# Attention scores as two 64-row groups on TensorE, with a weight ring one slot shorter

## The chip, the core and the metric

One core of one Trainium2 chip runs the whole kernel. The metric is device time in microseconds (us), from the start of the program to its end. The kernel before took 2022.97 us (median of three runs, 2017.64 to 2026.39).

## What is computed

Two layers of a transformer-like block over 512 latent and 256 context tokens, all in fp32. The part that matters here is the attention of the second and third head group. Each has four query heads of 64 and two key/value heads (kv) that two query heads each share; the heads that share one are called r = 0 and 1.

```
q, k = rope(rms_norm(heads(...)))             # per head; context tokens are not rotated
s = q k^T / 8                                 # latent tokens see latent and context keys
p = softmax(s)                                # group 1 (windowed): +-128 tokens around, context keys, a sink term
o = p v
```

Group 0 reads all 512 latent keys and the 256 context keys. Group 1 reads the latent keys of its own tile of 128 and of the neighbouring tiles (masked to the window), and the context keys. Context queries (layer 0 only) read context keys. Around the attention stand: modulation vectors from `w_mod` (24 matrix chunks, both layers, all in layer 0), an input projection `w_in`, convolutions, the output projection `w_out`, a router, and 32 experts per layer with `e_gate`, `e_up`, `e_down`.

## The kernel before

Tokens are cut into NT = 6 tiles of 128: four latent (0 to 3), two context (4, 5). Every engine has its own program, and semaphores order them.

**Weights.** A ring of SLOTS = 6 slots of 2 MB holds the weight chunks. SyncE (SP, lines 419 to 451) loads them strictly in the order of `CHUNKS`. Load j first waits until chunk j - 6, which held its slot, is used up (`used`, line 381). A `mod` chunk serves one step and a `w_in` chunk several: columns 768 (conv steps 0 to 3), columns 0 (steps 4 to 7), columns 512 (steps 8 and 9, 1 MB), columns 1280 (q/k/v of group 0, six units) and columns 1792 (group 1, six units). The order of steps in layer 0 is made in `steps_before_attention` (lines 67 to 80): four mod steps, ten conv steps, twelve qkv units, with mod steps dealt out beside them. Below, c0 to c9 are the conv steps in order, q0 to q11 the qkv units (q0 to q5 group 0, q6 to q11 group 1), and m0 to m23 the mod steps. Behind the chunks come nine expert pieces (three experts, three matrices each): six take the ring's slots, three take late slots.

**q and k.** `qkv_projection` (line 527) makes one tile's q, k, v. `rotate` (line 954, VectorE) normalises and rotates q and k into `qk`. Then `qk_transposes` (line 514) turns it, two transposes for q and one for k, into PSUM bank 6 or 7 by turns. `store_qk` (line 1006) copies to `qT` and `kT`: 128 partitions hold the two kv halves.

**Attention.** A unit is one query tile, group, kv and r. There are 48 units in layer 0 and 32 in layer 1, and two with the same kv make a pair. For a unit, TensorE runs `scores` (S): the 128-partition q against `kT_pad`, keys in which the other half's 64 partitions are zero. Lines 574 (latent keys), 576 (masks) and 577 (context keys) do this. VectorE takes the maximum (line 1040). ScalarE takes the exponential (1463). TensorE transposes (T, line 589), ScalarE copies them out (1478), and TensorE weighs the values (W, line 605, column tiles of 64) for both units of the pair, then turns the inverse sums (X, line 611). The order on TensorE is T(u), S(u+2), T(u+1), S(u+3), W, X, T(u+2). `kT_pad` is made by GpSimd memsets (1612, 1613) and four ScalarE copies (`pad_keys`, line 1480), two of them ahead of the first exponential and two behind the second.

**Experts.** Each block of up to 64 rows multiplies with its expert's three matrices (line 728), while SyncE reloads pieces (`reload`, line 405) as experts finish.

Of the kernel before, what the change touches and what calls it, by code (L numbers as in the profile page):

```python
# [13 lines left out]
P = 128  # L14
# [43 lines left out]
SLOTS = 6  # L58
SLOT = 4096
# [7 lines left out]
def steps_before_attention(layer):  # L67

    conv = [("conv", ct) for ct in CONV_ORDER]
    qkv = [("qkv", u) for u in range(QKV_UNITS)]  # L70
    if layer:
        return conv + qkv

    mod = [("mod", n) for n in range(12 * DEPTH)]
    steps, mod = mod[:MOD_FIRST], mod[MOD_FIRST:]
    for n, step in enumerate(conv + qkv):
        beside = 2 if n == 9 else 0 if n in (14, 15, 21) else 1
        steps += [step, *mod[:beside]]
        mod = mod[beside:]
    return steps  # L80
# [3 lines left out]
MOD_CONV = MOD_FIRST + 11  # L84
# [32 lines left out]
def chunk_slot(layer, j):  # L117

    return (TURN[layer] + j) % SLOTS


def piece_slot(layer, kind, third):

    n = PIECES.index((kind, third))
    return (TURN[layer] + len(CHUNKS[layer]) + n) % SLOTS if n < SLOTS else n

# [24 lines left out]
def hybrid_flow_block(nc, x, ctx_tokens, conditions, consts, smalls, rows, w_mod, w_in, w_out, w_router,  # L151
                      e_gate, e_up, e_down, out):
    stack = ExitStack()
    with stack:
# [42 lines left out]
        kT_pad = r1[:, 3072:6144].rearrange("p (g kv t) -> p g kv t", g=2, kv=2)  # L197
# [10 lines left out]
        qk_tmp = r2[:, 5088:5472]  # L208
        ln_std = r2[:, 3072:3072 + TOK]
# [11 lines left out]
        qT = r3[:, 1536:4608].rearrange("p (i t) -> p i t", i=4)  # L221
        kT = r3[:, 4608:6144].rearrange("p (i t) -> p i t", i=2)
# [61 lines left out]
        keys_zeroed, keys_padded = sems("keys_zeroed"), sems("keys_padded")  # L284
# [26 lines left out]
        def key_tiles(layer, group, i):  # L311

            if i >= XT:
                return 0, 0
            return (0, XT) if group == 0 else (max(i - 1, 0), min(i + 2, XT))
# [56 lines left out]
        def _(sp):  # L372
# [46 lines left out]
            for layer in range(DEPTH):  # L419
                n_chunks = len(CHUNKS[layer])  # L420
                for j in range(n_chunks):
                    if j >= SLOTS:
                        sp.wait_ge(*used(layer, j - SLOTS))
                    elif layer:
                        kind, third = PIECES[j]
                        if kind == "gate":
                            end = blocks_up_to(NE // HELD * HELD + third)
                        sp.wait_ge({"gate": gate_psum, "up": up_psum, "down": y_psum}[kind][layer - 1], end)
                        if j == 1:

                            for i in range(tiles_of(layer - 1)):
                                sp.wait_ge(y_loaded[i], 16 * layer)
                    load_chunk(layer, j)
                tiles = tiles_of(layer)
                for n, (kind, third) in enumerate(PIECES):

                    if n < SLOTS:
                        sp.wait_ge(*used(layer, n_chunks + n - SLOTS))
                    elif n == SLOTS:
                        sp.wait_ge(out_psum[layer], 2 * tiles)  # L440
                    elif n == SLOTS + 1:
                        sp.wait_ge(logit_psum[layer], tiles)
                        sp.wait_ge(h2_stored[layer], 16 * tiles)
                    else:
                        sp.wait_ge(route_done[layer], 1)
                    load_piece(layer, kind, third, third)
# [8 lines left out]
        def _(pe):  # L455
# [58 lines left out]
            def qk_transposes(layer, u):  # L514
# [3 lines left out]
                if u >= 2:  # L518
                    pe.wait_ge(qkT_ready, QKV_UNITS * layer + u - 1)
# [3 lines left out]
                for r in range(2 if is_full(layer, i) else 0):  # L523
                    pe.transpose(ps[:, 6 + u % 2, r * P:(r + 1) * P], qk[:, r * P:(r + 1) * P], ident)
                pe.transpose(ps[:, 6 + u % 2, 2 * P:3 * P], qk[:, 256:384], ident).then_inc(qkT_psum, 1)
# [32 lines left out]
            def scores(layer, u, unit):  # L558
                i, group, kv, r = unit
                a, b = key_tiles(layer, group, i)  # L560
                w = (b - a) * P
                q = qT[:, group * 2 + r, i * P:(i + 1) * P]
# [3 lines left out]
                if u == 0 or u == 4:  # L566
                    pe.wait_ge(keys_padded[layer], 2 * (group + 1))
                if w:
                    masks = []
                    if group == 1 and i > 0:  # L570
                        masks.append((512 - w, cst("mask_prev")))
                    if group == 1 and i < XT - 1:
                        masks.append((512 - P, cst("mask_next")))
                    pe.matmul(ps[:, bank, 512 - w:512], q, kT_pad[:, group, kv, a * P:b * P], start=True, stop=not masks)  # L574
                    for m, (at, mask) in enumerate(masks):
                        pe.matmul(ps[:, bank, at:at + P], ident, mask, start=False, stop=m == len(masks) - 1)
                pe.matmul(ps[:, bank + 1, 0:C], q, kT_pad[:, group, kv, S:TOK], start=True, stop=True).then_inc(s_psum[layer], 1)  # L577

            def attend(layer, u, unit, last_pT):
                i, group, kv, r = unit  # L580
                a, b = key_tiles(layer, group, i)
                tiles = list(range(a, b)) + list(range(XT, NT))
                w = (b - a) * P
# [3 lines left out]
                for n in range(len(tiles)):  # L587
                    at = 512 - w + n * P
                    mm = pe.transpose(ps_flat[:, 2048 + at:2048 + at + P], prob[:, u % 2, at:at + P], ident)  # L589
                mm.then_inc(pT_psum[layer], 1)  # L590

            def weigh(layer, pair, unit):
# [3 lines left out]
                a, b = key_tiles(layer, group, i)  # L596
                tiles = list(range(a, b)) + list(range(XT, NT))
                w = (b - a) * P
# [3 lines left out]
                for n, t in enumerate(tiles):  # L602
                    at = 512 - w + n * P
                    for r in range(2):
                        mm = pe.matmul(ps[r * HD:(r + 1) * HD, 6 + pair % 2, 0:P],  # L605
                                       v_tok[:, t, group * P + kv * HD:group * P + (kv + 1) * HD],
                                       probT[:, r, at:at + P], start=(n == 0), stop=(n == len(tiles) - 1),
# [208 lines left out]
        def _(ve):  # L816
# [137 lines left out]
            def rotate(layer, u):  # L954
# [17 lines left out]
                if full:  # L972
# [10 lines left out]
                if full:  # L983
# [20 lines left out]
                nc.vector.tensor_tensor(qk[:, :], qk[:, :], qk_tmp[:, :], ALU.add).then_inc(qk_ready, 1)  # L1004

            def store_qk(layer, u):
# [3 lines left out]
                bank = ps[:, 6 + u % 2, 0:384].rearrange("p (r t) -> p r t", r=3)  # L1010
                if is_full(layer, i):
                    own(nc.vector.tensor_copy(qT[:, group * 2:group * 2 + 2, i * P:(i + 1) * P], bank[:, 0:2, :]))
                nc.vector.tensor_copy(kT[:, group, i * P:(i + 1) * P], bank[:, 2, :]).then_inc(qkT_ready, 1)
# [19 lines left out]
            def unit_max(layer, u, unit):  # L1033

                i, group, kv, r = unit
                a, b = key_tiles(layer, group, i)
                w = (b - a) * P
                base = (u % 2) * 1024
                ve.wait_ge(s_psum[layer], u + 1)
                own(nc.vector.tensor_reduce(stat[:, u % 4, 3:4], ps_flat[:, base + 512 - w:base + TOK], AX.X, ALU.max))  # L1040
# [298 lines left out]
        def _(ac):  # L1339
# [113 lines left out]
            def unit_exp(layer, u, unit):  # L1453
                i, group, kv, r = unit
                a, b = key_tiles(layer, group, i)
                w = (b - a) * P
# [6 lines left out]
                nc.scalar.activation(prob[:, u % 2, 512 - w:TOK], ps_flat[:, base + 512 - w:base + TOK], ACT.Exp,  # L1463
# [7 lines left out]
            def unit_pT(layer, u, unit):  # L1471
                i, group, _, _ = unit
                a, b = key_tiles(layer, group, i)
                w = (b - a) * P
# [3 lines left out]
                nc.scalar.copy(probT[:, u % 2, 512 - w:TOK], ps_flat[:, 2048 + 512 - w:2048 + TOK]).then_inc(pT_ready[layer], 1)  # L1478

            def pad_keys(layer, group):  # L1480

                ac.wait_ge(qkT_ready, QKV_UNITS * layer + NT * (group + 1))
                ac.wait_ge(qkv_psum, QKV_UNITS * layer + QKV_UNITS)
                ac.wait_ge(keys_zeroed[layer], 4)
                for half, kv in ((slice(0, HD), 0), (slice(HD, P), 1)):
                    nc.scalar.copy(kT_pad[half, group, kv, :], kT[half, group, :]).then_inc(keys_padded[layer], 1)  # L1486
# [111 lines left out]
        def _(po):  # L1598
# [5 lines left out]
            for layer in range(DEPTH):  # L1604
# [5 lines left out]
                po.wait_ge(qkv_psum, QKV_UNITS * layer + QKV_UNITS)  # L1610
                for group in range(2):
                    nc.gpsimd.memset(kT_pad[HD:P, group, 0, :], 0.0).then_inc(keys_zeroed[layer], 1)
                    nc.gpsimd.memset(kT_pad[0:HD, group, 1, :], 0.0).then_inc(keys_zeroed[layer], 1)
# [156 lines left out]
```

## Time and profile before

| | us |
|---|---|
| median of three runs | 2022.97 |
| the profiled execution | 2015.68 |
| its span in the trace | 2013.9 |
| layer 0: steps before attention | 0 to 311 |
| layer 0: attention | 311 to 431 |
| layer 0: experts | 583 to 1081 |
| layer 1: attention | 1290 to 1385 |
| layer 1: experts | 1493 to 1974 |
| mean granted TensorE clock | 0.941 of 2.4 GHz |

The profile has a page (busy times, the span in slices, the chain of work that ended last) and a trace that answers by window, line or tile. PE is TensorE's matmul, PEld its weight loads, DVE is VectorE, ACT ScalarE, SPq SyncE's DMA queue. An fp32 matmul stands in the trace as two LDWEIGHTS and two MATMUL records. The chain gives, for each piece, its start, its duration and what it was, with "xN" records. It follows backwards what released each step, so work that is not on it was covered by other work.

### The profile page before, as it was taken

The page shows a single profiled execution, that of the slowest core. Times are in us where ns is not written, and L with a number is a line of the kernel's source. Part 1 is how long each engine was busy: PE and PEld are TensorE (multiplying, and loading weights), DVE is VectorE, ACT ScalarE, POOL GpSimd, SP SyncE. Part 2 cuts the span into 40 slices and gives each one's busy share as a digit, 9 for nine tenths or more (in the row PEclk, how much of TensorE's full clock was granted, in tenths as well). Part 3 has the DMA queues.
Part 4 walks back from the last instruction along what each step waited for, and adds up shares of the span by engine and source line. Part 5 has one row for each costly group of instructions (what it writes and reads, how often), then busy time and mean ns, then how long its engine had stood idle before and what let it go on. Part 6 is the DMA issues. An engine that isn't in the chain of part 4 may idle for free.

```text
span 2013.9 us, 26260 instructions
## 1 busy us (share of the span) xinstructions
PE 1688.8 (84%) x9986; PEld 997.4 (50%) x9987; DVE 625.6 (31%) x1413; ACT 357.3 (18%) x730; POOL 224.8 (11%) x342
## 2 busy tenths in 40 slices
PE   4999998989869889998793699799959879777771
PEld 2555445754645556654462344475536546444430
DVE  2093655652431111110013477563331101100003
ACT  3111116641200000000002301463210000000001
POOL 0000000000001111111113100000001111111113
PEclk9999998999869999999997799899969999999996
DMA  9459246001449999899998421100359999999994
GB/s 355 153 188 344 90 150 251 2 1 52 178 167 425 427 427 427 347 428 427 427 425 338 166 104 64 42 2 1 152 204 423 426 428 427 427 427 426 428 427 161
DMA packets 85416, 541.83 MB, mean 269 GB/s; under 512 B 6544, under 2 KB 9264, under 8 KB 60784
## 3 DMA queue, kind: packets, MB, share of 16 engines
q1 hardware_dynamic: 68016, 481.51, 58.3%
q0 software_dynamic: 17344, 59.55, 7.5%
q8 instruction: 38, 0.62, 0.1%
q14 instruction: 18, 0.15, 0.0%
HBM read 515.08 MB, written 25.95 MB: 269 GB/s over the span
## 4 chain that ended last, share of the span: by engine, by line
PE 61%; DMA 27%; DVE 6%; ACT 3%; issue 2%; POOL 0%; POOLq 0%; ACTq 0%; DVEq 0%
PE ps L728 21%; DMA ring<-in_e_up_dram 14%; DMA ring<-in_e_down_dram 10%; PE ps L510 9%; PE ps L539 7%; PE ps L679 6%; PE ps L574 2%; PE ps L469 2%; PE ps L605 2%; PE ps L589 2%; PE ps L577 2%; PE ps L721 1%; PE ps L478 1%; PE ps L658 1%; DMA xres<-in_ctx_tokens_dram 1%
## 5 line engine op out<-in xcount | busy, mean ns | idle before, releaser
L728 PE MATMUL ps<-ring,r 128*64 128x256 f32 (+1 forms) x3920 | 542.1, 432 | 92.6 <-DMA ring<-in_e_up_dram 38.7
L728 PEld LDWEIGHTS ps<-ring,r 128*64 128x64 f32 x3920 | 317.7, 140 | 303.2 <-issue 149.4
L1282 DVE TENSOR_TENSOR r<-r,ps 128x256 f32<-128x256 f32 x71 | 29.9, 421 | 830.1 <-PE ps L728 830.1
L728 PE MATMUL ps<-r 128*64 128x256 f32 (+1 forms) x1760 | 239.9, 426 | 35.9 <-DMA r<-in_e_up_dram 14.7
L728 PEld LDWEIGHTS ps<-r 128*64 128x64 f32 x1760 | 142.3, 138 | 125.9 <-issue 61.3
L510 PE MATMUL ps<-r,ring 128*128 128x512 f32 (+1 forms) x480 | 176.2, 527 | 3.3 <-ACT r L1373 3.3
L1537 ACT COPY r<-ps 128x512 f32<-128x512 f32 x71 | 41.6, 585 | 669.8 <-PE ps L728 669.8
L539 PE MATMUL ps<-ring,r 128*128 128x512 f32 (+1 forms) x384 | 155.9, 560 | 0.0
L679 PE MATMUL ps<-ring,r 128*128 128x512 f32 x320 | 141.5, 598 | 2.2 <-ACT r L1508 2.2
L510 PEld LDWEIGHTS ps<-r,ring 128*128 128x128 f32 x480 | 90.9, 191 | 92.0 <-issue 84.4
L539 PEld LDWEIGHTS ps<-ring,r 128*128 128x128 f32 x384 | 71.4, 190 | 79.1 <-issue 75.0
L947 DVE SCALAR_TENSOR_TENSOR r<-r,small 128x512 f32<-128x512 f32 (+1 forms) x180 | 104.6, 661 | 0.0
L679 PEld LDWEIGHTS ps<-ring,r 128*128 128x128 f32 x320 | 60.3, 192 | 73.4 <-issue 70.7
L1626 POOL DMA_INDIRECT r<-h_dram,idx_gather x75 | 74.1, 988 | 55.0 <-POOL idx_gather L1623 55.0
L1040 DVE TENSOR_REDUCE stat<-ps 128x1 f32<-128x768 f32 (+3 forms) x80 | 60.3, 754 | 59.8 <-PE ps L577 58.6
L1634 POOL DMA_INDIRECT y_dram<-r,idx_scatter x71 | 71.1, 1002 | 57.5 <-POOL idx_scatter L1631 54.9
L1623 POOL COPY idx_gather<-list_gather 128x1 uint32 (+1 forms) x75 | 13.7, 183 | 529.5 <-PE ps L721 468.7
L469 PE MATMUL ps<-ring,cond 128*32 128x512 f32 x384 | 49.6, 637 | 23.3 <-DMA ring<-in_w_mod_dram 23.3
L1463 ACT ACTIVATE r<-ps,stat 128x768 f32<-128x768 f32 (+3 forms) x80 | 60.2, 753 | 41.3 <-DVE stat L1043 26.3
L1534 ACT ACTIVATE r<-ps 128x256 f32<-128x256 f32 x71 | 27.2, 383 | 225.2 <-PE ps L728 225.1
L574 PE MATMUL ps<-r 128*128 128x512 f32 (+2 forms) x128 | 60.4, 555 | 7.8 <-ACT r L1486 7.8
L589 PE MATMUL ps<-const,r 128*128 128x128 f32 x368 | 55.9, 282 | 12.3 <-ACT r L1478 6.1
(184 smaller groups left out, 1453.6 us busy)
## 6 DMA issues: line engine op xcount, KB each, us to landing
ring<-in_e_gate_dram SPq DMA_DIRECT2D x44, 2048.0 KB
ring<-in_e_up_dram SPq DMA_DIRECT2D x44, 2048.0 KB, 42.4
ring<-in_e_down_dram SPq DMA_DIRECT2D x44, 2048.0 KB, 31.2
ring<-in_w_mod_dram SPq DMA_DIRECT2D x24, 2048.0 KB, 18.6
r<-in_e_gate_dram SPq DMA_DIRECT2D x20, 2048.0 KB
r<-in_e_up_dram SPq DMA_DIRECT2D x20, 2048.0 KB
r<-in_e_down_dram SPq DMA_DIRECT2D x20, 2048.0 KB
ring<-in_w_in_dram SPq DMA_DIRECT2D x8, 2048.0 KB, 20.8
```

Source lines behind the costliest of these rows:

```text
L469: mm = pe.matmul(ps[32 * g:32 * g + 32, mod_bank(n), :], cond[:, 2 * g + k, :], w[:, 2 * g + k, :], start=(k == 0), stop=(k == 1), tile_po ...
L510: mm = pe.matmul(ps[:, (ct % 2) * 2 + j, 0:tn], w[:, k, col:col + P], h1T[:, t0 // P:(t0 + tn) // P, k, :], start=(k == 0), stop=(k == KD ...
L539: mm = pe.matmul(ps[:, 4 + u % 2, c0:512], h1T[:, i, k, :], chunk_ap(layer, n)[:, k, c0:512], start=(k == 0), stop=(k == KD - 1))
L574: pe.matmul(ps[:, bank, 512 - w:512], q, kT_pad[:, group, kv, a * P:b * P], start=True, stop=not masks)
L589: mm = pe.transpose(ps_flat[:, 2048 + at:2048 + at + P], prob[:, u % 2, at:at + P], ident)
L679: mm = pe.matmul(ps[:, u % 2, :], catT[:, k, i * P:(i + 1) * P], w[:, k, :], start=(k == 0), stop=(k == 7))
L728: mm = pe.matmul(ps[g * B:(g + 1) * B, bank, 0:width], x, w[:, k, g * width:(g + 1) * width], start=(k == 0), stop=(k == last), tile_posit ...
L947: ins = nc.vector.scalar_tensor_tensor(out=dst, in0=src, scalar=wt, in1=dst, op0=ALU.mult, op1=ALU.add)
L1040: own(nc.vector.tensor_reduce(stat[:, u % 4, 3:4], ps_flat[:, base + 512 - w:base + TOK], AX.X, ALU.max))
L1463: nc.scalar.activation(prob[:, u % 2, 512 - w:TOK], ps_flat[:, base + 512 - w:base + TOK], ACT.Exp, bias=stat[:, u % 4, 0:1], scale=SCALE, ...
L1626: po.indirect_dma_start(out=xg, out_offset=None, in_=h2_dram[layer], in_offset=bass.IndirectOffsetOnAxis(ap=idx_gather[:, 0:1], axis=0),). ...
L1634: po.indirect_dma_start(out=y_dram[layer], in_=y_rows, in_offset=None, out_offset=bass.IndirectOffsetOnAxis(ap=idx_scatter[:, 0:1], axis=0 ...
```

## The change

- `scores` uses 64 rows of the array at a time. Even key tiles (0, 4, 2) lie in `kT` on the kv's own half of the partitions, odd ones (1, 5, 3) on the other half. Two matmuls, one per half, write neighbouring PSUM banks. `kT_pad`, its memsets and copies, and their semaphores go.
- Every q head must lie on both halves. `rotate` writes each head twice into `q_twice` (512 columns), there are four transposes for q instead of two, and `store_qk` copies 512 columns instead of 256. Banks 6 and 7 are used together by every unit, so a unit's transposes wait for the store of the unit before.
- `qT` needs twice the room. Group 1's goes into the ring's sixth slot. The ring rotates over five slots (`ROTATING = 5`): load j waits for chunk j - 5. Expert piece 5 goes into the sixth slot once all scores are made.
- The mod step that stood beside q10 stands beside c8.

```diff
+ROTATING = 5
-        beside = 2 if n == 9 else 0 if n in (14, 15, 21) else 1
+        beside = 2 if n in (8, 9) else 0 if n in (14, 15, 20, 21) else 1
-MOD_CONV = MOD_FIRST + 11
+MOD_CONV = MOD_FIRST + 12
 def chunk_slot(layer, j):
-    return (TURN[layer] + j) % SLOTS
+    return (TURN[layer] + j) % ROTATING
...
+        q_twice = r2[:, 5472:5984]
-        qT = r3[:, 1536:4608].rearrange("p (i t) -> p i t", i=4)
-        kT = r3[:, 4608:6144].rearrange("p (i t) -> p i t", i=2)
+        qT = [v.rearrange("p (h t) -> p h t", h=4) for v in (r3[:, 1536:4608], ring[:, SLOTS - 1, 0:3072])]
+        kT = r3[:, 4608:6144].rearrange("p (g s t) -> p g s t", g=2, s=2)
...
+        KEY_ORDER = ((0, 4, 2), (1, 5, 3))
...
-                    if j >= SLOTS:
-                        sp.wait_ge(*used(layer, j - SLOTS))
+                    if j >= ROTATING:
+                        sp.wait_ge(*used(layer, j - ROTATING))
...
-                for n, (kind, third) in enumerate(PIECES):
+                for n in (0, 1, 2, 5, 3, 4, 6, 7, 8):
+                    if n < ROTATING:
+                        sp.wait_ge(*used(layer, n_chunks + n - ROTATING))
+                    elif n == 5:
+                        sp.wait_ge(s_psum[layer], len(units_of(layer)))
...
-                if u >= 2:
-                    pe.wait_ge(qkT_ready, QKV_UNITS * layer + u - 1)
+                if u >= 1:
+                    pe.wait_ge(qkT_ready, QKV_UNITS * layer + u)
...
-                for r in range(2 if is_full(layer, i) else 0):
-                    pe.transpose(ps[:, 6 + u % 2, r * P:(r + 1) * P], qk[:, r * P:(r + 1) * P], ident)
+                for h in range(4 if is_full(layer, i) else 0):
+                    pe.transpose(ps[:, 6, h * P:(h + 1) * P], q_twice[:, h * P:(h + 1) * P], ident)
...
-                    pe.matmul(ps[:, bank, 512 - w:512], q, kT_pad[:, group, kv, a * P:b * P], start=True, stop=not masks)
-                pe.matmul(ps[:, bank + 1, 0:C], q, kT_pad[:, group, kv, S:TOK], start=True, stop=True).then_inc(s_psum[layer], 1)
+                for half, (tiles, order) in enumerate(zip(key_tiles(group, i), KEY_ORDER)):
+                    rows = slice((kv ^ half) * HD, (kv ^ half) * HD + HD)
+                    first, n = order.index(tiles[0]) * P, len(tiles) * P
+                    at = lo if half == 0 else 0
+                    mm = pe.matmul(ps[:, bank + half, at:at + n], qT[group][rows, r * 2 + kv, i * P:(i + 1) * P],
+                                   kT[rows, group, half, first:first + n], start=True,
+                                   stop=not masks or half != (i + 1) % 2, tile_position=(rows.start, 0))
+                for m, (at, mask) in enumerate(masks):
+                    mm = pe.matmul(ps_flat[:, bank * 512 + at:bank * 512 + at + P], ident, mask, ...
...
-                nc.vector.tensor_tensor(heads[:, nh - 2:nh, :], bank[:, nh - 2:nh, :],
-                                        qk_rstd[:, 4:6].unsqueeze(2).to_broadcast([P, 2, HD]),
-                                        ALU.mult).then_inc(qk_scaled, 1)
+                for kv in range(2):
+                    ins = nc.vector.tensor_scalar(heads[:, nh - 2 + (kv ^ i % 2), :], bank[:, nh - 2 + kv, :],
+                                                  qk_rstd[:, 4 + kv:5 + kv], None, ALU.mult)
+                ins.then_inc(qk_scaled, 1)
...
-                nc.vector.tensor_tensor(qk[:, :], qk[:, :], qk_tmp[:, :], ALU.add).then_inc(qk_ready, 1)
+                own(nc.vector.tensor_tensor(both, twice(qk[:, 0:256]), twice(qk_tmp[:, 0:256]), ALU.add))
+                nc.vector.tensor_tensor(qk[:, 256:384], qk[:, 256:384], qk_tmp[:, 256:384], ALU.add).then_inc(qk_ready, 1)
...
             def attention(layer):
-                pad_keys(layer, 0)
                 unit_exp(layer, 0, units[0])
                 unit_exp(layer, 1, units[1])
-                pad_keys(layer, 1)
```

## Rows read from the trace of the kernel before

**Rows 1.** The page: busy times by engine, and the chain's shares by engine.

```profile
PE 1688.8 (84%) x9986; PEld 997.4 (50%) x9987; DVE 625.6 (31%) x1413; ACT 357.3 (18%) x730; POOL 224.8 (11%) x342
PE 61%; DMA 27%; DVE 6%; ACT 3%; issue 2%; POOL 0%; POOLq 0%; ACTq 0%; DVEq 0%
```

**Rows 2.** Windows: length, busy (instructions) of PE, PEld, DVE, ACT, POOL; clock; DMA.

```profile
311.00:400.00 89.00, 85.76 (x647) 63.67 (x648) 52.86 (x132) 52.35 (x106) 0.00 (x0) 0.94 0.30 122
1493.00:1974.00 481.00, 399.67 (x2836) 228.58 (x2832) 47.61 (x99) 33.23 (x67) 76.64 (x131) 0.98 0.98 415
```

**Rows 3.** The chain in layer 0's attention: start, duration, what.

```profile
342.21 0.66 PE ps L589 x6
342.87 0.86 PE ps L574 x2
343.73 0.43 PE ps L577 x2
346.34 1.46 PE ps L605 x24
347.81 0.26 PE ps L611
368.99 1.46 PE ps L605 x24
```

**Rows 4.** Timeline there, VectorE and ScalarE: start, duration, what, idle before.

```profile
344.20 0.96 DVE L1040 TENSOR_REDUCE stat<-ps 128x1 f32<-128x768 f32 x1 [1.39 <-PE ps L577]
345.09 0.80 ACT L1478 COPY r<-ps 128x768 f32<-128x768 f32 x1 [1.03 <-PE ps L589]
347.56 0.90 ACT L1463 ACTIVATE r<-ps,stat 128x768 f32<-128x768 f32 x1 [0.78 <-DVE stat L1043]
```

**Rows 5.** The chain through layer 0's conv steps and qkv units.

```profile
91.75 10.52 PE ps L510 x32
103.06 1.85 PE ps L469 x16
104.91 10.52 PE ps L510 x32
...
170.70 10.52 PE ps L510 x32
...
187.47 7.06 PE ps L539 x16
...
235.46 6.99 PE ps L539 x16
...
242.46 7.92 DMA ring<-in_w_mod_dram
```

**Rows 6.** Timeline of TensorE among the experts: the same work twice.

```profile
950.22 3.67 PE L728 MATMUL ps<-ring,r 128*64 128x256 f32 x32 [1.38 <-DMA ring<-in_e_gate_dram]
955.81 5.36 PE L728 MATMUL ps<-ring,r 128*64 128x256 f32 x32 [1.92 <-DMA ring<-in_e_up_dram]
```

**Rows 7.** The chain in layer 1's qkv units.

```profile
1225.49 0.22 PE ps L524 x2
...
1225.82 6.87 PE ps L539 x16
```

**Rows 8.** Timeline of VectorE in `store_qk` and `rotate`, layer 1.

```profile
1233.05 0.42 DVE L1012 COPY r<-ps 128x256 f32<-128x256 f32 x1 [1.00 <-PE ps L525]
1237.37 0.56 DVE L1004 TENSOR_TENSOR r<-r 128x384 f32<-128x384 f32 x1
```

**Rows 9.** Timeline at the start of layer 0's attention.

```profile
309.19 1.67 ACT L1486 COPY r<-r 64x768 f32<-64x768 f32 x2
310.62 0.28 DVE L986 TENSOR_TENSOR r<-r,row 128x128 f32<-128x128 f32 x1
319.04 1.51 PE L589 MATMUL ps<-const,r 128*128 128x128 f32 x6 [3.16 <-ACT r L1463]
```

**Rows 10.** The chain at the start of layer 1's attention.

```profile
1288.13 0.29 ACT qk_std L1430
1297.87 1.51 PE ps L589 x6
```

More of the change, by code:

```diff
@@ L309, in streams_of, with key_tiles, key_span, key_columns @@
             return [(0, 0, S), (1, S, C)][:2 if layer == 0 else 1]
[L311 to L315, printed above, removed]
+        KEY_ORDER = ((0, 4, 2), (1, 5, 3))
+        def key_tiles(group, i):
+            near = range(XT) if group == 0 else range(max(i - 1, 0), min(i + 2, XT))
+            seen = [*(near if i < XT else ()), *range(XT, NT)]
+            return [[t for t in order if t in seen] for order in KEY_ORDER]
+        def key_span(group, i):
+            even, odd = key_tiles(group, i)
+            return 512 - len(even) * P, 512 + len(odd) * P
+        def key_columns(group, i):
+            lo, _ = key_span(group, i)
+            even, odd = key_tiles(group, i)
+            return [(t, lo + n * P) for n, t in enumerate(even + odd)]
         def units_of(layer):
@@ L434, in _ @@
                 tiles = tiles_of(layer)
-                for n, (kind, third) in enumerate(PIECES):
-                    if n < SLOTS:
-                        sp.wait_ge(*used(layer, n_chunks + n - SLOTS))
-                    elif n == SLOTS:
+                for n in (0, 1, 2, 5, 3, 4, 6, 7, 8):
[3 more added lines that the diff above has]
+                        sp.wait_ge(s_psum[layer], len(units_of(layer)))
+                    elif n == 6:
                         sp.wait_ge(out_psum[layer], 2 * tiles)
-                    elif n == SLOTS + 1:
+                    elif n == 7:
                         sp.wait_ge(logit_psum[layer], tiles)
@@ L559, in scores @@
                 i, group, kv, r = unit
-                a, b = key_tiles(layer, group, i)
-                w = (b - a) * P
-                q = qT[:, group * 2 + r, i * P:(i + 1) * P]
+                lo, _ = key_span(group, i)
                 bank = (u % 2) * 2
@@ L565, in scores @@
                     pe.wait_ge(exp_done[layer], u - 1)
[L566 to L573, printed above, removed]
-                    pe.matmul(ps[:, bank, 512 - w:512], q, kT_pad[:, group, kv, a * P:b * P], start=True, stop=not masks)
-                    for m, (at, mask) in enumerate(masks):
-                        pe.matmul(ps[:, bank, at:at + P], ident, mask, start=False, stop=m == len(masks) - 1)
-                pe.matmul(ps[:, bank + 1, 0:C], q, kT_pad[:, group, kv, S:TOK], start=True, stop=True).then_inc(s_psum[layer], 1)
+                masks = []
+                for t, at in key_columns(group, i):
+                    if group == 1 and t < XT and abs(t - i) == 1:
+                        masks.append((at, cst("mask_prev" if t < i else "mask_next")))
+                for half, (tiles, order) in enumerate(zip(key_tiles(group, i), KEY_ORDER)):
[6 more added lines that the diff above has]
+                for m, (at, mask) in enumerate(masks):
+                    mm = pe.matmul(ps_flat[:, bank * 512 + at:bank * 512 + at + P], ident, mask,
+                                   start=False, stop=m == len(masks) - 1)
+                mm.then_inc(s_psum[layer], 1)
             def attend(layer, u, unit, last_pT):
                 i, group, kv, r = unit
-                a, b = key_tiles(layer, group, i)
-                tiles = list(range(a, b)) + list(range(XT, NT))
-                w = (b - a) * P
                 pe.wait_ge(exp_done[layer], u + 1)
@@ L586, in attend @@
                     pe.wait_ge(*last_pT)
-                for n in range(len(tiles)):
-                    at = 512 - w + n * P
-                    mm = pe.transpose(ps_flat[:, 2048 + at:2048 + at + P], prob[:, u % 2, at:at + P], ident)
+                for _, at in key_columns(group, i):
+                    mm = pe.transpose(ps_flat[:, 2048 + at:2048 + at + P], prob[:, u % 2, at - P:at], ident)
                 mm.then_inc(pT_psum[layer], 1)
@@ L595, in weigh @@
                 i, group, kv, _ = unit
-                a, b = key_tiles(layer, group, i)
-                tiles = list(range(a, b)) + list(range(XT, NT))
-                w = (b - a) * P
+                columns = key_columns(group, i)
                 pe.wait_ge(pT_ready[layer], 2 * pair + 2)
@@ L601, in weigh @@
                     pe.wait_ge(o_ready[layer], pair - 1)
-                for n, t in enumerate(tiles):
-                    at = 512 - w + n * P
+                for n, (t, at) in enumerate(columns):
                     for r in range(2):
@@ L606, in weigh @@
                                        v_tok[:, t, group * P + kv * HD:group * P + (kv + 1) * HD],
-                                       probT[:, r, at:at + P], start=(n == 0), stop=(n == len(tiles) - 1),
+                                       probT[:, r, at - P:at], start=(n == 0), stop=(n == len(columns) - 1),
                                        tile_position=(0, r * HD))
@@ L1009, in store_qk @@
                 ve.wait_ge(qkT_psum, QKV_UNITS * layer + u + 1)
-                bank = ps[:, 6 + u % 2, 0:384].rearrange("p (r t) -> p r t", r=3)
                 if is_full(layer, i):
-                    own(nc.vector.tensor_copy(qT[:, group * 2:group * 2 + 2, i * P:(i + 1) * P], bank[:, 0:2, :]))
-                nc.vector.tensor_copy(kT[:, group, i * P:(i + 1) * P], bank[:, 2, :]).then_inc(qkT_ready, 1)
+                    own(nc.vector.tensor_copy(qT[group][:, :, i * P:(i + 1) * P],
+                                              ps[:, 6, :].rearrange("p (h t) -> p h t", h=4)))
+                first = KEY_ORDER[i % 2].index(i) * P
+                nc.vector.tensor_copy(kT[:, group, i % 2, first:first + P], ps[:, 7, 0:P]).then_inc(qkT_ready, 1)
             def ln_centre(layer):
@@ L1035, in unit_max @@
                 i, group, kv, r = unit
-                a, b = key_tiles(layer, group, i)
-                w = (b - a) * P
+                lo, hi = key_span(group, i)
                 base = (u % 2) * 1024
                 ve.wait_ge(s_psum[layer], u + 1)
-                own(nc.vector.tensor_reduce(stat[:, u % 4, 3:4], ps_flat[:, base + 512 - w:base + TOK], AX.X, ALU.max))
+                own(nc.vector.tensor_reduce(stat[:, u % 4, 3:4], ps_flat[:, base + lo:base + hi], AX.X, ALU.max))
                 settle()
@@ L1454, in unit_exp @@
                 i, group, kv, r = unit
-                a, b = key_tiles(layer, group, i)
-                w = (b - a) * P
+                lo, hi = key_span(group, i)
                 base = (u % 2) * 1024
@@ L1472, in unit_pT @@
                 i, group, _, _ = unit
-                a, b = key_tiles(layer, group, i)
-                w = (b - a) * P
+                lo, hi = key_span(group, i)
                 ac.wait_ge(pT_psum[layer], u + 1)
@@ L1477, in unit_pT @@
                     ac.wait_ge(o_psum[layer], u // 2)
[L1478 to L1486, printed above, removed]
+                nc.scalar.copy(probT[:, u % 2, lo - P:hi - P], ps_flat[:, 2048 + lo:2048 + hi]).then_inc(pT_ready[layer], 1)
             def attention(layer):
                 units = units_of(layer)
-                pad_keys(layer, 0)
                 unit_exp(layer, 0, units[0])
                 unit_exp(layer, 1, units[1])
-                pad_keys(layer, 1)
                 for u in range(0, len(units), 2):
@@ L1608, in _ @@
                 po.dma_start(router_w[:, :, :], w_router[layer].rearrange("(k p) n -> p k n", p=P)).then_inc(router_in, 16)
[L1610 to L1613, printed above, removed]
                 for i in range(tiles):
```

17 lines of the change are left out of this document (11 added, 6 removed).

## The prediction, made before the changed kernel was run

> **What bounds the kernel now.** I read the page first. TensorE is busy 84% of the span and carries 61% of the chain, and DMA carries 27% [rows 1]. Then I read windows. In layer 0's attention TensorE is busy 85.8 of 89 us, VectorE and ScalarE some 52 each [rows 2]. So the attention is TensorE's, and the chain through it is nearly TensorE alone. A tile of four pairs takes 368.99 - 346.34 = 22.65 us [rows 3]. The steps before it are TensorE's as well, conv step after conv step [rows 5]. The expert stage is bound by the loads: DMA share 0.98 [rows 2]. By the order of SyncE's waits all nine pieces held ahead can land before it starts, before and after. Its first reload waits for the first expert, so a shift of all that comes before shifts the end one for one. That includes layer 0's, since layer 1 starts when layer 0's experts end. I therefore add up what happens before each expert stage.
>
> **Scores, what is removed.** 512 columns of fp32 take 0.86 us and 256 take 0.43 [rows 3], 0.215 per key tile of 128. If the two halves run side by side, a unit costs its longer half: group 0 falls from six tiles to three (-0.64), group 1 from four to two or from five to three (-0.43), context queries from two to one (-0.21). Layer 0 has 16 units of each, layer 1 has 16 + 16. That is 20.6 + 17.2 = 37.8 us of TensorE time less.
>
> Do tiles run side by side? No row tile is in this trace, but column tiles are. W's twelve matmuls of 128 columns would take 12 x 0.213 = 2.56 us one after another and take 1.46 [rows 3]. A mod step's eight matmuls of 512 columns on four column tiles would take 6.8 and take 1.85 [rows 5]. I take row tiles to do the same.
>
> **Scores, what is added.** The same rows show a price for going from the whole array to tiles and back. Fully side by side W is 1.28, so 0.18 over. X is one transpose and takes 0.26, where six take 0.66, so 0.15 over [rows 3]. The mod step is 1.71 fully side by side, so 0.14 over, and the projection behind a mod step takes 7.06 against 6.87 without one, 0.19 over [rows 5, 7]. I take 0.16 us a switch. A pair now switches twice (into W, out of it). After the change a group 0 or context pair switches five times, a group 1 pair six times, because its masks use the whole array. That is 80 more switches in layer 0 and 56 in layer 1: 12.8 + 9.0 = 21.8 us given back.
>
> The Trainium skill has a rule against this change here: "TensorEngine Tiling (Array Packing)", Key Properties, says that changing the tiling mode drains TensorE. The price of 0.14 to 0.19 beside tiled work agrees. The page gives no price for row tiles.
>
> The ledger so far is -16, but TensorE will no longer be alone on the chain. T(u+1) cannot start before ScalarE has copied T(u) out, 0.80 us plus some 0.18 of signals, and S(u+2), which covered that with 1.29, is now 0.64 plus two switches. There is also a loop from S to the maximum (0.96), the exponential (0.90), the copy (0.80) and the next T [rows 4]. I replayed one layer's order by hand with these durations: each instruction starts when its engine is free and what it waits for is done, 0.14 us from ScalarE to TensorE and 0.04 elsewhere. The replay gives 22.6 us a tile for the kernel before, as measured. For the kernel after it gives 21.4. Over the layers it gives -4.4 and -4.5: **-9 us** (-20 if a switch costs nothing, 0 if it costs 0.25).
>
> **Start of attention.** The padding copies of 1.67 us stand between the last square root and the first S [rows 9]. The last unit's transposes stand behind S(0) and S(1), at the half clock, and the first maximum stands behind these. After the change S(0) and S(1) run earlier. The last transposes start when VectorE is done (310.9 now, some 311.5 after). Transposes at half clock 0.8, copies 0.9, amplitude 0.3, maximum 1.1 and exponential 1.1 bring T(0) to 315.7 instead of 319.04. Group 1's padding copies delayed the first copy out by another 0.8. That is -4.1. In layer 1, T(0) stands 9.7 us behind the last square root [rows 10]. After: VectorE's end and one transpose 1.7, maximum 1.1, exponential 1.1, rest 0.4 put it 4.3 behind one that comes 0.5 later, -4.9. Sum **-9 us**. GpSimd's memsets were hidden and save nothing.
>
> **The ring of five.** Here is the cost. The w_in chunks are each five apart in the order (chunks 4, 9, 14, 19, 24), so all fall into one slot, and the load of each waits until the one before is used up. Its first matmul is next on TensorE, and every later load queues behind it on SyncE. Before, the chunk that waited so was a mod chunk, needed one whole unit later. What such a load takes from an idle queue is seen once: q5 ends at 242.46, five loads go out, and the first is there 7.92 us later [rows 5]. What covers it:
> - c4 started 104.91 - 102.27 = 2.64 us after c3's end [rows 5], so it waits 5.3 us.
> - c8 has the same cover for a chunk of half the size. At 415 GB/s [rows 2] 1 MB less is 2.5 us less, so it lands in some 5.4: 2.8 us.
> - q0 started 187.47 - 181.22 = 6.25 us after c9's end, behind two mod steps: 1.7 us.
> - q6 started right behind q5 and its transposes (0.33): 7.6 us.
>
> Together **+17.4 us** (9 if a load takes 5.5 us, 20 if it takes 8.6). VectorE's work goes on under the waits but was not late.
>
> After a wait TensorE may run at 1.2 GHz. Two like pieces of expert work take 3.67 and 5.36 us, the second after 1.92 us of waiting [rows 6], 1.7 lost. I count 2.0 for the waits before c4 and q6: **+4.0** (0 to 7).
>
> **The moved mod step.** Beside q10 it was covered by VectorE's layer norm, which the last units wait for. Beside c8 it is second in a row, as m14 was behind m13: q0 came 6.25 us after c9 where c4 came 2.64 after c3 [rows 5]. **+3.6 us.**
>
> **q and k.** A transpose is 0.11 [rows 7]. Layer 0 has two more in each unit. Ten units lie ahead of the layer norm; one is under the wait before q6 and one in the start above, so 8 x 0.22 = +1.8. In layer 1, seven: +1.5. VectorE's 256 columns take 0.42 and 384 take 0.56 [rows 8], some 0.27 more for 256 columns more. Store +0.27, final add +0.33, k scaled in two +0.15. That makes 0.75 a unit, hidden under the next projection of 6.87, except at layer 1's q3, where the short projection of a context tile follows and VectorE already ends the wait: +0.75. Together **+4.1 us**. The wait of the transposes for the store before is satisfied six us early. Layer 1's five first chunks are loaded ahead and its sixth is w_out, needed much later: nothing. Piece 5 lands at the start of the output projection: nothing.
>
> **Sum.** 17.4 + 4.0 + 3.6 + 4.1 - 9 - 9 = +11.1 us on the profiled execution's 2015.7, so 2026.8. That execution lies 7 us under the median of the three runs. On the median 2023.0 the forecast is 2034.
>
> **The rivals.**
> - A: switches to row tiles are free. Body -20 instead of -9: 0, so 2023. For it: a 64-row tile's weights could load while the other half still works. Against: all four places where tiles begin or end show the price. 24%.
> - B: a row-tile switch costs 0.25, because two loads of 128-column weights lie open where W's have 64. Body 0: +20, 2043. 15%.
> - C: the change doesn't do what it says, and the two halves run one after the other. No stream is saved and the switches stay. The replay gives +16 instead of -9: +36, 2059. It decides from the first unit, S of group 0 then being 1.3 + 0.3 us. Against: column tiles overlap. 9%.
> - D, the other side: loads land faster, in 5.5 us, because the 7.92 included four loads behind it, and the clock does not fall, and A holds too: 9 + 0 + 3.6 + 4.1 - 9 - 20 = -12, so 2011. 10%.
>
> The Trainium skill, "TensorE: Matmul & The Clock Gate", Part 3, gives a model that speaks for A: tiles on different rows start about 4 ns apart and weight loads of one row group run under the other's matmuls. By it a score pair would cost its longer half alone and A's 2023 would be the time. No row tile in this trace shows it.
>
> **Chances and range.** The forecast has 42%, of which 26 lie over +10 us and 16 under. A measurement here can tell about 0.5%, 10 us. Slower: 26 + 15 + 9 = 50%. Same: 16 + 20 of A + 4 of D = 40%. Faster: 4 of A + 6 of D = 10%. The range leaves out C and D: from A less 5 us to B plus 7, 2018 to 2050.
>
> **What would show it.** In the profile after: SyncE's w_in loads go out at the ends of c3, c7, c9 and q5, and TensorE waits for them 5.3, 2.8, 1.7 and 7.6 us. S of group 0 takes about 0.64 us plus 0.15 to 0.35 from T's end to the next T. A tile of attention takes about 21.4 us. T(0) stands about 5 us behind the last square root. The prediction is wrong if those waits are missing or twice as long, or if S takes 1.3 us or more (C) or tiles take 19.7 (A).

## The result and the profile after

The changed kernel takes 2037.18 us (median of five runs, 2030.08 to 2043.68) against 2022.97 before. The ratio is 1.0075, with a 95% interval from 1.0043 to 1.0107. It is slower by 14 us, where 11 were forecast. Its profiled execution took 2030.08 us, 14.4 more than that of the kernel before, so the traces can account for the difference.

The page: busy times and the chain by engine, as in [rows 1].

```profile
PE 1677.3 (83%) x10058; PEld 972.9 (48%) x10059; DVE 642.3 (32%) x1453; ACT 350.7 (17%) x722; POOL 218.9 (11%) x334
PE 58%; DMA 28%; DVE 8%; ACT 3%; issue 2%; POOL 0%; POOLq 0%; ACTq 0%; DVEq 0%
```

TensorE is busy 11.5 us less and yet the span is 14.4 longer. The chain through layer 0's conv steps and qkv units says where, beside [rows 5]:

```profile
90.34 10.53 PE ps L526 x32
100.89 7.74 DMA ring<-in_w_in_dram
108.67 13.59 PE ps L526 x32
...
161.76 5.34 DMA ring<-in_w_in_dram
167.15 10.59 PE ps L526 x32
178.52 1.90 PE ps L485 x16
182.13 1.85 PE ps L485 x16
183.99 10.53 PE ps L526 x32
194.53 8.76 DMA ring<-in_w_in_dram
203.34 8.83 PE ps L555 x16
...
260.97 7.79 DMA ring<-in_w_in_dram
268.81 8.58 PE ps L555 x16
```

Four loads of `w_in` stand on the chain that were not there before. They start when c3, c7, c9 and q5 end. In front of c4, c8, q0 and q6 TensorE waits 5.17, 2.78, 2.58 and 7.32 us for them. Two of these waits in the timeline of TensorE (the wait is the number in brackets):

```profile
167.15 10.59 PE L526 MATMUL ps<-r,ring 128*128 128x512 f32 x32 [2.78 <-DMA ring<-in_w_in_dram]
203.34 3.68 PE L555 MATMUL ps<-ring,r 128*128 128x512 f32 x4 [2.58 <-DMA ring<-in_w_in_dram]
```

Behind three of the loads the same work takes longer: conv step c4 13.59 for 10.52, projection q0 8.83 for 7.06, and projection q6 8.58 for 6.87 (it has no mod step in front, as in [rows 7]). The granted clock over these stretches was 0.78, 0.81 and 0.83, so part of each ran at 1.2 GHz. Behind the load before c8 it was 1.00, and c8 lost nothing (10.59). Between c8 and c9 stand two mod steps.

The chain in the attention, beside [rows 3] (L602 is T, L588 the scores with two halves, L592 the masks, L615 is W):

```profile
366.42 0.85 PE ps L602 x6
367.27 0.85 PE ps L588 x4
368.12 0.04 issue
368.16 1.53 PE ps L615 x24
...
370.61 0.84 PE ps L588 x3
371.44 0.64 PE ps L592 x4
...
389.85 1.53 PE ps L615 x24
```

Scores of group 0 took 0.86 + 0.43 = 1.29 and take 0.85. Those of group 1 with two masks took 0.65 + 0.44 + 0.43 = 1.52 and take 0.84 + 0.64 = 1.48. A tile of four pairs took 22.65 and takes 389.85 - 368.16 = 21.69. TensorE was busy through all of the 22.65; of the 21.69 it is busy 21.01 and waits 0.68, most of it for ScalarE's copy before a transposing step (0.52 before the one at 388.12).

The start of attention and layer 1's qkv units, beside [rows 7, 9, 10]:

```profile
324.24 4.87 DVE r L1048
343.81 1.51 PE ps L602 x6
...
1254.73 1.10 PE ps L540 x4
...
1256.05 4.58 PE ps L555 x16
...
1299.44 3.27 DVE r L1048
1313.63 1.51 PE ps L602 x6
```

L1048 is the layer norm's reciprocal, a fixed point ahead of the attention; the same line of the kernel before started at 295.67 and 1278.55. The table cuts both chains at such points:

| stretch | before | after | difference |
|---|---|---|---|
| up to c0, layer 0 | 53.00 | 51.58 | -1.4 |
| c0 to the layer norm, layer 0 | 242.67 | 272.66 | +30.0 |
| layer norm to T(0) | 23.37 | 19.57 | -3.8 |
| T(0) to the end of attention | 112.26 | 107.39 | -4.9 |
| output projection and routing, to the first expert | 151.68 | 147.28 | -4.4 |
| first expert to c0 of layer 1 | 551.23 | 551.06 | -0.2 |
| c0 to the layer norm, layer 1 | 144.34 | 149.90 | +5.6 |
| layer norm to T(0) | 19.32 | 14.19 | -5.1 |
| T(0) to the last W | 85.72 | 83.43 | -2.3 |
| last W to the first expert | 108.69 | 109.83 | +1.1 |
| first expert to the end | 521.6 | 521.4 | -0.2 |

The expert stages take the same, so a shift in front of them comes out whole at the end. Each trace is one execution. Two of the rows differ from kernel to kernel also where the kernels do the same: the time up to c0 lies between 51.6 and 59.6 us in the eight traces of this study, and that from the end of attention to the first expert in layer 0 between 147.3 and 151.7.

### The profile page after: what moved, and what is told of

Same layout as the page of the kernel before. It is cut to its first block, busy times and chain, and to the rows that moved or that the text cites. A ratio compares the mean times of both kernels' runs of the same rounds, so it can differ in the third digit from the quotient of the medians.

```text
span 2028.3 us, 26445 instructions
## 1 busy us (share of the span) xinstructions
PE 1677.3 (83%) x10058; PEld 972.9 (48%) x10059; DVE 642.3 (32%) x1453; ACT 350.7 (17%) x722; POOL 218.9 (11%) x334
## 4 chain that ended last, share of the span: by engine, by line
PE 58%; DMA 28%; DVE 8%; ACT 3%; issue 2%; POOL 0%; POOLq 0%; ACTq 0%; DVEq 0%
PE ps L738 21%; DMA ring<-in_e_up_dram 14%; DMA ring<-in_e_down_dram 10%; PE ps L526 9%; PE ps L555 7%; PE ps L689 6%; PE ps L588 2%; PE ps L485 2%; PE ps L615 2%; PE ps L602 2%; DMA ring<-in_w_in_dram 1%; PE ps L731 1%; PE ps L668 1%; DVE stat L1060 1%; PE ps L494 1%
## 5 line engine op out<-in xcount | busy, mean ns | idle before, releaser
L738 PEld LDWEIGHTS ps<-ring,r 128*64 128x64 f32 x3920 | 312.3, 139 | 307.9 <-issue 139.0
L555 PE MATMUL ps<-ring,r 128*128 128x512 f32 (+1 forms) x384 | 160.3, 572 | 9.9 <-DMA ring<-in_w_in_dram 9.9
L1620 POOL DMA_DIRECT2D h_dram<-r x10 | 5.4, 540 | 876.2 <-DVE r L1133 876.2
L602 PE MATMUL ps<-const,r 128*128 128x128 f32 x368 | 56.1, 282 | 17.1 <-ACT r L1496 10.2
```

Source lines behind the costliest of these rows:

```text
L555: mm = pe.matmul(ps[:, 4 + u % 2, c0:512], h1T[:, i, k, :], chunk_ap(layer, n)[:, k, c0:512], start=(k == 0), stop=(k == KD - 1))
L738: mm = pe.matmul(ps[g * B:(g + 1) * B, bank, 0:width], x, w[:, k, g * width:(g + 1) * width], start=(k == 0), stop=(k == last), tile_posit ...
```

## The experiments

**Ring of six with the row groups.** The h1T tiles come free one by one while group 1's units run, and the doubled q of tile i is written when tiles 0 to i+1 are free. So the ring can keep six slots.

```diff
-ROTATING = 5
+ROTATING = 6
...
-        beside = 2 if n in (8, 9) else 0 if n in (14, 15, 20, 21) else 1
+        beside = 2 if n == 9 else 0 if n in (14, 15, 21) else 1
...
-        qT = [... (r3[:, 1536:4608], ring[:, SLOTS - 1, 0:3072])]
+        qT = [r3[:, 1536:4608].rearrange("p (h t) -> p h t", h=4),
+              r1[:, 0:3072].rearrange("p (i h t) -> p h i t", i=NT, h=4)]
...
-        prob = r1[:, 0:1536] ... probT = r1[:, 1536:3072]
+        prob = r1[:, 3072:4608] ... probT = r1[:, 4608:6144]
...
-                for n in (0, 1, 2, 5, 3, 4, 6, 7, 8):
+                for n in range(9):
...
```

> The change with a ring of six again: group 1's q goes into the columns that the h1T tiles leave free, the order of mod steps and of pieces is that of before. Theory (the ring of five, with the moved mod step and the clock behind the waits, costs some 25 us and the row groups save some 11): 2037 - 25 = 2012 us, ratio to before 0.994; c4, c8, q0 and q6 start without a wait for DMA. Rival (the loads were hidden well enough, and the row groups with the doubled queries are themselves the loss): about 2035, ratio 1.006.

Measured: 2009.51 us, ratio to before 0.9950 (0.9935 to 0.9966). In its chain c3's successors and q6 come without a load between:

```profile
103.22 1.85 PE ps L484 x16
105.08 10.52 PE ps L525 x32
...
236.49 6.97 PE ps L554 x16
244.01 6.87 PE ps L554 x16
```

c8 and q0 start without a load in front as well. The theory holds and the rival falls. The change without its ring is 10 us faster than before. By the two ratios (1.0075 and 0.9950) the ring with its mod step cost about 25 us. In the stretch where it acts, from c0 to layer 0's layer norm, the traces have 272.66 with it and 244.58 without: 28.1.

**Ring of five with its mod step, on the kernel before.** There is no row group and no second q. The order of the expert pieces is that of the change.

```diff
+ROTATING = 5
...
-        beside = 2 if n == 9 else 0 if n in (14, 15, 21) else 1
+        beside = 2 if n in (8, 9) else 0 if n in (14, 15, 20, 21) else 1
...
-                        sp.wait_ge(*used(layer, j - SLOTS))
+                        sp.wait_ge(*used(layer, j - ROTATING))
...
```

> The kernel before with nothing of the change but the ring of five, the moved mod step and the order of the pieces. Theory: 17.4 us of waits, 4 of clock, 3.6 for the mod step: +25, 2048 us, ratio 1.012. Rival: the waits overlap with what VectorE and ScalarE need anyway, ratio at most 1.003.

Measured: 2049.68 us, ratio 1.0140 (1.0122 to 1.0159). Its chain has the same four loads as the changed kernel:

```profile
106.67 7.77 DMA ring<-in_w_in_dram
...
166.03 5.36 DMA ring<-in_w_in_dram
171.44 12.28 PE ps L513 x32
...
200.53 9.31 DMA ring<-in_w_in_dram
...
266.49 7.80 DMA ring<-in_w_in_dram
```

So the ring with its mod step costs 28 us without a single row group in the kernel, 3 more than expected. In the stretch from c0 to the layer norm it costs 271.35 - 242.67 = 28.7 here and 28.1 in the changed kernel. The two views agree. The rival falls.

c8 shows how unsteady the clock term is: TensorE waited 2.80 us before it here and 2.78 in the changed kernel, and it took 12.28 here and 10.59 there.

What the two halves of this edit cost each is shown in part only. The next experiment prices the moved step with a ring of six. But the move also makes q0's `w_in` chunk number 19; with the step in its old place it is number 18, and in a ring of five its load would wait for a mod chunk instead of chunk 14. No run has the ring of five with the step in its old place.

**The moved mod step alone.**

```diff
-        beside = 2 if n == 9 else 0 if n in (14, 15, 21) else 1
+        beside = 2 if n in (8, 9) else 0 if n in (14, 15, 20, 21) else 1
...
-MOD_CONV = MOD_FIRST + 11
+MOD_CONV = MOD_FIRST + 12
```

> The kernel before with only one mod step moved from beside q10 to beside c8, ring of six. Theory: +3.6 us, ratio 1.002, the time from c8 to q0 longer by 3.6 and nothing given back behind q9. Rival: the step only changes places, 0.

Measured: 2022.63 us, ratio 1.0016 (0.9997 to 1.0034). The interval takes in no change, so the time alone decides nothing. The chain has the 3.6 us in their place, between the end of c8 at 174.62 and c9:

```profile
164.10 10.52 PE ps L510 x32
175.40 1.90 PE ps L469 x16
179.01 1.85 PE ps L469 x16
180.87 10.52 PE ps L510 x32
```

c9 starts 6.25 us after c8's end, where one mod step leaves 2.64 [rows 5]. From the start of c8 to the layer norm it is 305.88 - 164.10 = 141.78, and was 295.67 - 157.54 = 138.13 before: 3.65 more, so nothing is given back behind q9. The rival falls in the trace.

**One row group only.** All key tiles stay on the kv's own 64 partitions. Nothing is padded and nothing can run side by side; the order of masks and context keys is that of the change.

```diff
-                q = qT[:, group * 2 + r, i * P:(i + 1) * P]
+                rows = slice(kv * HD, (kv + 1) * HD)
+                q = qT[rows, group * 2 + r, i * P:(i + 1) * P]
-                    pe.matmul(ps[:, bank, 512 - w:512], q, kT_pad[:, group, kv, a * P:b * P], ...)
+                    pe.matmul(ps[:, bank, 512 - w:512], q, kT[rows, group, a * P:b * P], ...,
+                              tile_position=(rows.start, 0))
...
-                pad_keys(layer, 0)
...
-                pad_keys(layer, 1)
...
```

> The kernel before without padded keys: q and keys of one kv are taken from its 64 partitions, all key tiles on the same row group, so nothing can run side by side; no memsets, no padding copies. It prices the switches. Theory (a switch between the whole array and 64-row tiles costs some 0.2 us, 136 more of them): the attention from the first transposes on is longer by 10 us a layer, its start shorter by 4 to 5 a layer: +11 us, ratio 1.005. Rival (switches to row tiles are free): only the start is left, -9 us, ratio 0.9955, attention body as before.

Measured: 2036.01 us, ratio 1.0087 (1.0066 to 1.0108). The chain (L591 is T, L571 and L575 are scores, L578 masks, L607 is W):

```profile
348.56 1.05 PE ps L571 x2
349.62 0.43 PE ps L575 x2
350.05 1.46 PE ps L607 x24
...
352.42 0.84 PE ps L571 x2
353.26 0.43 PE ps L575 x2
353.69 0.64 PE ps L578 x4
...
375.19 1.46 PE ps L607 x24
```

Latent keys and masks of group 1 in the kernel before:

```profile
348.72 0.65 PE ps L574 x2
349.37 0.44 PE ps L576 x4
```

512 columns take 1.05, not 0.86 as on the whole array [rows 3]: 0.19 for the way in. The 256 columns behind them, on the same row group, take 0.43 as before, so it is the way in that costs and not the columns. Four mask records take 0.64 for 0.44: 0.20 for the way out. A tile takes 375.19 - 350.05 = 25.14 against 22.65. That is 2.5 us for the 14 more switches of a tile, 0.18 each, with TensorE alone on the chain. Switches to row tiles are not free, and rival A falls. The step from this kernel to row groups side by side is 25.14 to 21.69 a tile. So the two halves do overlap, and rival C falls too.

The whole kernel was expected at +11 us, ratio 1.005, and came out at 1.0087, above that. From the first W to the end of attention it is 10.3 us longer in layer 0 and 10.1 in layer 1, as expected for the switches. Ahead of that it went otherwise. From the layer norm to T(0) layer 0 gained 1.2 us and layer 1 4.7, where 4 to 5 each were expected. From T(0) to the first W both layers took 8.69 at a granted clock of 0.50, where the kernel before took 6.87 and 5.58.

**ScalarE copies q.** This is on top of the ring of six.

```diff
                 nc.scalar.activation(qk_tmp[:, c0:384], ps[:, 4 + u % 2, c0:384], ACT.Square).then_inc(qk_square, 1)
+                if u >= 1 and on_act(layer, u - 1):
+                    ac.wait_ge(qkT_psum, QKV_UNITS * layer + u)
+                    nc.scalar.copy(qT..., ps[:, 6, :].rearrange("p (h t) -> p h t", h=4)).then_inc(q_stored, 1)
```

> e1_ring6 with ScalarE, not VectorE, copying the 512 columns of q out of PSUM for all units but the last. Theory (in layer 1 the doubled q makes VectorE late at q3 and at q9, where the short projection of a context tile follows, and the wait drops the clock: +2.9 us that the prediction did not have): the two waits shrink by 0.5 to 0.7 each, the clock may stay up, 2 to 4 us less in layer 1's qkv units and at most 1 in layer 0: 4 us under e1_ring6, ratio to before 0.993. Rival (the clock falls there whatever the length of the wait, and ScalarE's copy delays its square root): within 1 us of e1_ring6, 0.995.

Measured: 2005.98 us, ratio 0.9941 (0.9919 to 0.9963). That of the ring of six lies within this interval, so the last 3 us rest on the traces. From layer 1's c0 to its layer norm the ring of six takes 149.98 us and this kernel 146.52. In layer 0 the same stretch takes 244.58 and 243.97. What follows the wait at q3, first with VectorE's copy, then with ScalarE's:

```profile
1233.31 1.02 PE ps L539 x4
...
1234.54 4.67 PE ps L554 x16
```

```profile
1231.32 0.66 PE ps L550 x4
...
1232.09 3.46 PE ps L565 x16
```

TensorE waited 1.70 us there instead of 2.30, and the projection of 256 columns took 3.46 instead of 4.67: the granted clock was 1.00 for 0.71. In all eight traces the short projection at this place took 3.46 behind waits of 1.51 and 1.70, and 4.58 or 4.67 behind the two waits of 2.30. The theory holds in the trace. Of the 3.5 us about 2 are won at q3 and 1.5 in the last units before the layer norm. This kernel has the lowest median of the study.

**Row groups for group 0 only.** Group 1 goes back to one q and padded keys, and the rest is as in the kernel above.

```diff
+                if group == 1:
+                    q = qT[1][:, r, i, :]
+                    pe.matmul(ps[:, bank, lo:512], q, kT_pad[:, kv, near[0] * P:(near[-1] + 1) * P], ...)
+                    ...
+                    pe.matmul(ps[:, bank + 1, 0:C], q, kT_pad[:, kv, S:TOK], start=True, stop=True).then_inc(s_psum[layer], 1)
+                    return
...
```

> e5 with row groups and doubled queries for group 0 alone; group 1 keeps the single q and zero-padded keys, padded by ScalarE behind the first two exponentials. Theory (with some 0.2 us a switch, row groups gain nothing in group 1, where a unit with two masks takes 1.48 against 1.52 us, and lose on its context queries): group 1's transposes and stores go back (about 2 us in each layer's qkv units), its attention units stay equal within 0.1 us, the padding copies cost up to 1 us a layer: 2 us under e5, ratio 0.992. Rival (the row groups earn in group 1 too, through the loop from scores to the next transposes): 3 or more us over e5, ratio 0.995 or higher.

Measured: 2009.66 us, ratio 0.9959 (0.9943 to 0.9975). Against the expectation it is not faster than the kernel before it; whether it is slower the overlapping intervals leave open. The trace has the padding copies on the chain, ahead of layer 1's T(1), and a tile of 369.25 - 347.37 = 21.88:

```profile
347.37 1.53 PE ps L652 x24
...
369.25 1.53 PE ps L652 x24
...
1291.47 0.72 ACT r L1553
...
1292.21 0.83 ACT r L1553
```

In group 1 the row groups are thus worth 0.2 us a tile, next to nothing, as the theory had it. It failed in both other terms. The transposes and stores that go back were to bring 2 us a layer ahead of the layer norm, and the traces have 243.43 for 243.97 in layer 0 and 146.75 for 146.52 in layer 1. The two copies take 1.67 us and hold up ScalarE's first copy out: from layer 1's layer norm to its first W it is 20.89 for 19.21, though in layer 0 it is 25.52 for 25.74. The first W behind it then ran at the lower clock in both layers, 2.76 and 2.18 for 1.53. The measured 3.7 us over the kernel before it lie where the rival put them (3 or more, ratio 0.995 or higher), but not for its reason, since the tiles are nearly equal. Of the 8.1 us between the two profiled spans 4.7 stand ahead of c0, where the kernels are the same.

## Why the prediction was right

The sum was +11.1 and the measured difference is +14.2, inside the range and with the sign forecast. The mechanisms named were the right ones: the waits of the ring outweigh what the row groups save. That the number is so near is in part luck. In the table the rows for which the sum has a term (from c0 to the end of attention in layer 0, and from c0 to the last W in layer 1) come to +19.5, 8.4 above the forecast. The other rows come to -5.1, most of it the two of -1.4 and -4.4, and bring the difference of the traces back to +14.4. Term by term:

- **The waits of the ring.** Forecast 5.3, 2.8, 1.7 and 7.6, together 17.4. Measured as waits of TensorE: 5.2, 2.8, 2.6 and 7.3, together 17.9. Only q0's was off, since that load took 8.76 us.
- **The clock behind them.** Forecast 4.0 for two waits. The slowed conv step and the two slowed projections lost 3.1, 1.8 and 1.7: 6.6. The wait of 2.6 us before q0 cost as much as the one of 7.3 before q6, and the one of 2.8 before c8 cost nothing. The term is too small because the shorter waits were taken to be harmless, though [rows 6] had shown the loss behind 1.9 us, and because c4 lost 3.1 and not 2.0.
- **The mod step.** Forecast 3.6; the trace has 6.25 - 2.64 = 3.6, in the changed kernel as in the experiment.
- **q and k.** In layer 0 what is left of +30.0 after 17.9, 6.6 and 3.6 is 1.9, forecast 1.8. The ring of six, where these waits are missing, is 244.58 - 242.67 = 1.9 over the kernel before in the same stretch. In layer 1 about 2.8 were forecast ahead of the layer norm, and 5.6 were measured. The mechanism was right, VectorE late at q3. The clock that fell behind that wait was missed: 1.10 and 4.58 for a transposing step and a projection that take 0.44 and 3.46 at full clock. q9 was missed as well: the same short projection follows there, and from q8 on VectorE is on the chain up to the layer norm. The kernel with ScalarE's copy gives 3.5 of the two back.
- **Start of attention.** Forecast -4.1 and -4.9 (with 0.8 of the first behind T(0)); measured -3.8 and -5.1 up to T(0).
- **The body.** Forecast -9 from the replay at 0.16 us a switch, 21.4 us a tile. Measured -4.9 and -2.3. From T(0) to the first W layer 0 is 2.1 us shorter and layer 1 0.6 longer. The clock has a part in both: 0.68 after 0.59 before in layer 0, 0.51 after 0.73 before in layer 1. Behind the first W it is -2.8 and -2.9, with tiles of 21.69 us. The switch was mis-sized: 0.19 to 0.21 on the way in and 0.20 on the way out, with weights of 128 columns, where 0.14 to 0.19 were read from column tiles of 64 and 32. The kernel with one row group gave 0.18 on average. With 14 more switches a tile, 0.02 more for each is the 0.3 us by which the forecast tile of 21.4 was too short. The replay was not done again with that price, so this last step is an estimate. The Trainium skill, "TensorEngine Tiling (Array Packing)", Key Properties, says that changing the mode drains the engine. The price beside row tiles agrees with it, though no run separates a drain from weight loads that lie open.
- **Context queries** were taken at 0.21 less a unit and three switches more a pair, about even. Two of their pairs took 429.67 - 418.08 = 11.59 us and take 449.58 - 437.99 = 11.59. VectorE and ScalarE are on the chain there.
- **Not in the sum:** -1.4 up to c0 and -4.4 in layer 0's output stage. In the latter the first transposes and the first projection took 3.68 and 8.33 us in the trace before, at the lower clock, and 1.96 and 7.03 in the trace after. The row groups are not the cause. The kernel with only the moved mod step has none of them and also takes 1.96 and 7.03, with 147.82 for the stretch. The ring of six has all of them and takes 151.13. Up to c0 the two kernels do the same steps. I take both rows for the chance of the execution.

The Trainium skill, "TensorE: Matmul & The Clock Gate", Part 3, has tiles on different rows cost little more than one of them. For the streams of a unit that is borne out: three tiles of keys on each half take 0.85, of which 0.64 are the columns of one half. By that model alone the score would take 0.64, an estimate. The measurement decides: the 0.21 over it, a quarter of the time, is the way between whole array and tiles.

Rivals: A falls with the one-row-group kernel. B's price (0.25) was too high, and the truth lies between it and the forecast. C falls with the measured overlap. D falls with loads of 2 MB that took 7.7 to 8.8 us.

## What to carry to other kernels

A ring of buffers is sized by the longest-held entry: if the entries that stay for several steps stand as far apart as the ring is long, each waits for the one before, and one slot less costs whole loads, here some 25 us (with the moved mod step) for 10 gained. Before giving a slot away, write down which load waits for which use. Splitting small matmuls over tiles pays per switch between whole array and tiles: count the switches, and look in the chain at what else was hidden under the time that the matmuls no longer take.

## What was not expected of the hardware

A wait of two to three us in front of TensorE can cost as much as one of seven. The waits of 2.58 before q0 and of 7.32 before q6 both left the next projection partly at 1.2 GHz, 1.8 and 1.7 us lost. But it need not: the wait of 2.78 before c8 cost nothing in one kernel, and one of 2.80 at the same place cost 1.8 us in another. So the length of the wait does not settle it, and a forecast needs a range there. At layer 1's q3 the eight traces were more regular: waits of 1.51 and 1.70 kept 2.4 GHz, the two of 2.30 did not. There a copy moved to ScalarE made the wait 0.6 us shorter, and 3.5 us were won in all before the layer norm.
